# Hybrid RWKV-7 / short-convolution / expert block on one core: the w_o product in three f32r passes over blocks split as they arrive, and expert rows fetched two rounds ahead

## The reference, cut to what matters

```python
# 1024 tokens + 16 meta tokens = 1040 rows, D_MODEL 1024, 32 experts, top 4
x_n = _rmsnorm(h, ln1_g)
proj = x_n @ w_in
y_a = _rwkv7_branch(...)          # recurrence over 8 heads of 64
y_b = _short_conv_branch(...)
merged = sigmoid(gate_a) * y_a + sigmoid(gate_b) * y_b
h = h + merged @ w_o              # (1040, 1024) @ (1024, 1024)
xf = _rmsnorm(h, ln2_g)
logits = xf @ w_router + b_router
top_v, top_i = lax.top_k(logits, 4)
gates = softmax(top_v)
# per block of 128 rows that chose expert e:
gt = minimum(xb @ w_e_gate[e] + b_e_gate[e], 7)
up = clip(xb @ w_e_up[e] + b_e_up[e], -7, 7)
act = (up + 1) * (gt * sigmoid(1.702 * gt))
y = (act @ w_e_down[e] + b_e_down[e]) * wts
h = h + sum of the four y of each token
out = _rmsnorm(h, lnf_g)[16:]
```

## Time and profile before

| | us |
|---|---|
| median of 3 runs | 3091.75 (3083.33 to 3095.08) |
| the profiled execution | 3067.25 |
| its span in the profile | 3065.6 |
| PE busy | 2798.6 (91%) |
| DVE busy | 1789.7 (58%) |
| ACT busy | 1361.6 (44%) |
| POOL busy | 514.2 (17%) |

### The profile page before, as it was taken

How to read it: one execution, slowest core, us unless ns; L and a number is a source line. 1 busy time by engine, 2 the same in 40 slices (tenths; PEclk the granted TensorE clock), 3 DMA queues, 4 the chain that set the end, 5 groups by cost and what they waited for, 6 DMA issues and landing times.

```text
span 3065.6 us, 55893 instructions
## 1 busy us (share of the span) xinstructions
PE 2798.6 (91%) x21371; PEld 2340.7 (76%) x21371; DVE 1789.7 (58%) x1990; ACT 1361.6 (44%) x1501; POOL 514.2 (17%) x511
## 2 busy tenths in 40 slices
PE   7999999999998999796899999999899999999993
PEld 6797878878898999443688878888777777777772
DVE  3456546464422121143576776767788888888885
ACT  2423232232211111032565666665666666666664
POOL 1010101010000000123132323232222212222220
PEclk9999999999999999897899999999999999999996
DMA  3000000000012110522677868777988888988887
GB/s 105 21 2 15 8 8 15 2 22 1 28 41 56 41 41 21 156 67 70 230 280 257 282 248 283 257 281 264 352 324 323 323 327 330 353 331 329 327 331 245
DMA packets 143212, 536.25 MB, mean 175 GB/s; under 512 B 17633, under 2 KB 71239, under 8 KB 90125
## 3 DMA queue, kind: packets, MB, share of 16 engines
q1 hardware_dynamic: 122925, 492.74, 43.4%
q0 software_dynamic: 20192, 42.08, 5.6%
HBM read 500.35 MB, written 34.42 MB: 174 GB/s over the span
## 4 chain that ended last, share of the span: by engine, by line
PE 71%; DMA 14%; issue 7%; DVE 3%; POOL 2%; ACT 2%; POOLq 1%; SPq 0%; ACTq 0%; DVEq 0%
PE bank L839 30%; PE bank L1958 8%; PE bank L1959 7%; PE bank L1960 7%; DMA x_rows<-hn_d,next_t 6%; DMA next_t<-slot_d 5%; PE bank L1967 5%; PE bank L1871 4%; PE bank L1936 2%; PE bank L835 2%; POOL mid_t L1496 2%; PE bank L915 2%; DMA wo_t<-in_w_o 1%; PE bank L1946 1%; PE bank L2028 1%
## 5 line engine op out<-in xcount | busy, mean ns | idle before, releaser
L1789 DVE TENSOR_TENSOR w_lo<-raw_first,w_hi 128x2048 fp32r<-128x2048 f32 x275 | 618.3, 2283 | 73.7 <-ACT w_hi L1584 73.6
L1584 ACT ACTIVATE w_hi<-raw_first 128x2048 fp32r<-128x2048 f32 x276 | 529.5, 1919 | 228.1 <-DMA raw_first<-in_w_e_up 63.4
L1958 PE MATMUL bank<-w_hi,x_hi 128*128 128x512 f32 x1088 | 434.0, 399 | 2.4 <-ACT yo_rows L1632 2.4
L1959 PE MATMUL bank<-w_lo,x_hi 128*128 128x512 f32 x1088 | 425.1, 391 | 0.0
L1960 PE MATMUL bank<-w_hi,x_lo 128*128 128x512 f32 x1088 | 424.8, 390 | 0.0
L1789 DVE TENSOR_TENSOR w_lo<-raw_rest,w_hi 128x2048 fp32r<-128x2048 f32 x136 | 307.8, 2282 | 0.2
L1584 ACT ACTIVATE w_hi<-raw_rest 128x2048 fp32r<-128x2048 f32 x136 | 260.8, 1917 | 100.8 <-PE bank L1994 43.4
L839 PE MATMUL bank<-xm_hi,ring_hi 128*128 128x260 f32 x896 | 261.9, 292 | 16.2 <-DVE dz L791 8.2
L839 PE MATMUL bank<-xm_lo,ring_hi 128*128 128x260 f32 x896 | 255.0, 285 | 0.0
L839 PE MATMUL bank<-xm_hi,ring_lo 128*128 128x260 f32 x896 | 255.0, 285 | 0.0
L1958 PEld LDWEIGHTS bank<-w_hi,x_hi 128*128 128x128 f32 x1088 | 204.8, 188 | 51.2 <-issue 10.4
(11 more groups left out here) (364 smaller groups left out, 4706.3 us busy)
## 6 DMA issues: line engine op xcount, KB each, us to landing
raw_first<-in_w_e_up SPq DMA_DIRECT2D x138, 1024.0 KB, 5.9
raw_first<-in_w_e_gate SPq DMA_DIRECT2D x70, 1024.0 KB, 6.4
raw_rest<-in_w_e_gate SPq DMA_DIRECT2D x70, 1024.0 KB, 5.6
raw_first<-in_w_e_down SPq DMA_DIRECT2D x68, 1024.0 KB, 6.3
raw_rest<-in_w_e_down SPq DMA_DIRECT2D x68, 1024.0 KB, 8.7
ring<-in_w_in SPq DMA_DIRECT2D x40, 512.0 KB, 3.9
hn_d<-hn SPq DMA_DIRECT2D x10, 416.0 KB
h_d<-h_all SPq DMA_DIRECT2D x10, 416.0 KB
```

Source lines behind the costliest of these rows:

```text
L1584: nc.scalar.activation(w_hi[:, j % NRING, :, :], raw_piece(j), ACT.Copy).then_inc(hi_done, 1)
L1789: nc.vector.tensor_tensor(w_lo[:, j % NRING, :, :], raw_piece(j), w_hi[:, j % NRING, :, :].bitcast(f32), ALU.subtract).then_inc(lo_done, 1)
L1958: nc.tensor.matmul(ps[:, :], hi, w_hi[:, slot, k, :], start=start and k == 0, stop=False)
L1959: nc.tensor.matmul(ps[:, :], hi, w_lo[:, slot, k, :], start=False, stop=False)
```

## The change

- w_o: `mT` and w_o are both split in a high and a low f32r part, and `project_out` does three products for each of the eight channel blocks. w_o is split block by block (q = 0 to 15, a block is 128 channels by 512 columns); the first six blocks are loaded before the end of the gates into room that is free then, the other ten after it in two transfers ahead of `h_all`. ACT does the high parts (`split_wo_hi`, `split_m_hi`), DVE the low ones; those of tiles 2 to 9 of `mT` are done two tiles ahead, within the loop over tiles.
- The bias rows are laid out over 96 partitions (1024 elements each) in place of 32 (3072), and go out in six transfers in place of two.
- The padding (`make_pads`) is moved from the start of the w_o stage into the first `gather`, between the issue of the slot reads and the wait for them.
- `gather(1)` is done ahead of the loop, and in round r POOL does `gather(r + 2)`, behind the copy to `slot_t` and ahead of `get_biases(r + 1)` and the scatter. It waits for `xT_ps` of round r + 1.

```diff
+    WO_EARLY = 6
+    m_hi = wo("m_hi", [128, 2, KT, TP], f32r)
+    m_lo = wo("m_lo", [128, 2, KT, TP], f32r)
...
+        sp.dma_start(wo_early, w_o[:, 0:WO_EARLY, 0:512]).then_inc(wo_in[0], 16)
         sp.wait_ge(gate_mul, 3 * KT * NCH + 6)
-        sp.dma_start(wo_t[:, :, 0:512], w_o[:, :, 0:512]).then_inc(wo_in[0], 16)
+        sp.dma_start(wo_late[:, 0:KT - WO_EARLY, :], w_o[:, WO_EARLY:KT, 0:512]).then_inc(wo_in[1], 16)
+        sp.dma_start(wo_late[:, KT - WO_EARLY:, :], w_o[:, :, 512:1024]).then_inc(wo_in[2], 16)
         for t in range(NT):
-            if t == 2:
-                sp.dma_start(wo_t[:, :, 512:1024], w_o[:, :, 512:1024]).then_inc(wo_in[1], 16)
...
-        nc.gpsimd.memset(xo_rows, 0.0).then_inc(pads_done, 1)
-        nc.gpsimd.memset(bias_t.bitcast(f32), 0.0).then_inc(pads_done, 1)
...
         def gather(r, wide):
...
+            if isinstance(r, int) and r == 0:
+                make_pads()
             pool.wait_ge(idx_in[0], r * 16 + 16)
...
         gather(0, True)
         get_biases(0)
+        pool.wait_ge(rows_in[0], 16)
+        pool.wait_ge(rows_in[1], 16)
+        nc.gpsimd.tensor_copy(mid_t, next_t).then_inc(mid_kept, 1)
+        nc.gpsimd.tensor_copy(mid_ov, next_ov).then_inc(mid_kept, 1)
+        pool.wait_ge(mid_kept, 2)
+        pool.wait_ge(xT_ps[3], 1)
+        gather(1, True)
         pool.wait_ge(h_out, 16 * NT)
         for first, last, wide in ((0, n_wide, True), (n_wide, rounds, False)):
             with pool.Fori(first, last) as r:
-
-                pool.wait_ge(rows_in[0], r * 16 + 16)
...
-                pool.wait_ge(xT_ps[3 if wide else 1], r + 1)
-                gather(r + 1, wide)
...
+                pool.wait_ge(rows_in[0], r * 16 + 32)
...
+                pool.wait_ge(xT_ps[3 if wide else 1], r + 2)
+                gather(r + 2, wide)
...
+        act.wait_ge(gate_mul, 3 * KT * 4 + 6)
+        split_m_hi(0)
+        for q in range(KT):
+            split_wo_hi(q)
+        split_m_hi(1)
+        for q in range(KT, 2 * KT):
+            split_wo_hi(q)
...
             for k in range(KT):
-                ins = nc.tensor.matmul(bank[2 * (t % 2) + n][0:TP, :], mT[:, k, TP * t:TP * (t + 1)],
-                                       wo_t[:, k, 512 * n:512 * (n + 1)], start=k == 0, stop=k == KT - 1)
+                if t == 0:
+                    pe.wait_ge(wo_m_lo_done, WO_SPLITS['w', KT * n + k])
+                nc.tensor.matmul(ps, m_hi[:, t % 2, k, :], wo_hi[:, n, k, :], start=k == 0, stop=False)
+                nc.tensor.matmul(ps, m_hi[:, t % 2, k, :], wo_lo(KT * n + k), start=False, stop=False)
+                ins = nc.tensor.matmul(ps, m_lo[:, t % 2, k, :], wo_hi[:, n, k, :], start=False, stop=k == KT - 1)
```

## The result

The changed kernel takes 3007.63 us (median of 4 runs, 3003.55 to 3011.05), the kernel before 3087.54 (4 runs beside it on the same chip, 3081.65 to 3095.08). The ratio is 0.9739, with a 95% interval of 0.9711 to 0.9767: 80 us less, where 21 less was forecast. The two profiled executions lie closer together, 3067.25 and 3007.41, spans 3065.6 and 3005.8: 60 us.

A forecast was written before the change was run, and what follows sets the result against it. PE was taken as the bound in wide rounds, narrow rounds and w_o, stopping once a narrow round for x_rows. The terms -34 - 87 + 100 = -21 us on a median of 3091.75 gave 3071 us, range 2990 to 3140.

The forecast's parts named there:

- Narrow rounds, 87 forecast: Rows two rounds ahead remove the stall; less 0.3 us for biases and 0.6 for DMA, 4.1 us saved in 21 rounds.
- The stall: Narrow rounds: PE stops 3.34 us before x_part for x_rows, then loses 1.7 to low clock; 5.0 us a round.
- Wide rounds, 100 forecast: Biases read behind gather(r + 2) make PE stop 6.0 us, plus 1.7 of low clock; 7.7 us lost in 13 rounds.
- POOL's chain: Wide rounds, behind part f = 3: 1.5 us load, G 7.5, 1.5 expert load, 5.7 landing; 16.2 against 10.2 available.
- G: Time in POOL's wide-round chain for slot reads and both gathers: taken as 7.5 us, 6.0 at the least, 11.6 longest.
- rival 2: Wide rounds: next to no bias stop, small transfers land at once, rounds stay at 52 us; 2971 us, chance 0.07.
- Rival 1: Wide rounds: short bias stop of 3.2 us, G 6.0, costing 42 to 64 us; 3013 to 3035 us, chance 0.15.
- Rival 3: Wide rounds: POOL's chain with G 11.6 and landing 5.8, stop of 10.2 us, 171 lost; 3142 us, chance 0.16.
- Rival 4: Narrow rounds gain only 2 us, held at 39 by DMA or biases; 42 saved, 3116 us, chance 0.12.
- w_o, 34 forecast: w_o stage: tile 0's transposes 11 us earlier, then 17 halves saving 1.43 each, 24 us; 34 saved (28 to 40).
- its first low part at 1256.6: w_o start: half 1 waits for the second late transfer, there at about 1255.5; PE stops another 4 us.
- is covered by the next half of 5.4 and the logits, with over a us to spare: w_o tiles: the norm, some 5 us behind a tile's last product, stays hidden despite 0.9 us more DVE and ACT work.

The follow-up runs named there:

- the second pair of profiles: The kernel before and the changed kernel, both run again unaltered with profiles on the experiments' chips: 3066.69 us and 3017.8 us.
- the extra products: Changed kernel plus 18 f32r products that nothing reads, on PE in wide rounds before the wait for bias_t: 3003.03 us, ratio 0.9795.
- the w_o part alone: Kernel before plus the w_o work, bias layout and moved padding, with POOL's loop left one round ahead: 3044.14 us, ratio 0.9912.

## Why the prediction was right, and where its terms were off

The three mechanisms were there, each with its sign and at its place; the sizes were off, and most of each error has a name. Forecast was -34 - 87 + 100 = -21; on the chips of the experiments the whole is -50, in the first two profiles -60. So the way and the wide range of 2990 to 3140 came true, the size did not: 3007.63 lies below the 3035 to 3105 that the forecast itself was given. Two of the three errors point the same way, 26 us more from the narrow rounds and 18 less lost in the wide ones, and w_o, 9 short, took back a part of them.

**Narrow rounds, 87 forecast, 113 measured** (5.38 x 21; from the first product of round 13 on the two profiles differ by 112.6). The stall went with its full 5.0 us. I took off 0.3 for the biases and 0.6 for DMA at its limit; neither came. The DMA share is 1.00 and PE still runs every one of 600 us. The biases are issued some 7.1 us behind the slot read (2273.35 and 2266.26), while the sum for them had 7.8 + 1.0 + 1.5 = 10.3: the gather follows the slot read after 5.9 us instead of 7.8, and the load of the expert's number hardly shows. Why the slot read lands sooner isn't shown. The rest is the period itself. I took the one of the earlier trace rows, 40.95, and the mean over 20 rounds is 41.29.

**Wide rounds, 100 forecast, 81.5 measured** (83.0 in the second pair of profiles; 6.7 and 6.9 us a round). POOL's chain was 1.5 + 7.5 + 1.5 + 5.7 = 16.2. In the round shown it is 1.4 to the slot read's issue, 6.5 from there to the issue of the biases (1552.05 and 1558.53), which holds the load of the expert's number too, and 7.4 for the landing: 15.3, and a stop of 4.94. So G and the load, taken as 7.5 + 1.5 = 9.0, were the terms too large by 2.5: G was at its lower bound of 6.0, and the load lies mostly beside the gather's issue. The landing was 1.7 longer than the 5.7 I took and 1.3 longer than the longest of the earlier trace rows. The thirteenth read, for round 13, is needed in a narrow round and made PE wait only 1.3 us, so there were 12 stops to charge and not 13; their mean is (57.8 - 1.3) / 12 = 4.7 us. The clock cost what I took, 1.7: the extra products gave back 1.6 of it. Stop and clock together are 6.3 of the 6.7 us a round; the other 0.4 I can't place to one wait.

The Trainium skill (DMA: Bandwidth & Descriptors, Anatomy of one DMA), by which the biases would land in 2.06 us, is not what is mostly seen: they took 7.4 in the chain above, and rival 2 fell with it. One read, in round 11, did land after 2.31 us, near it, with no weights under way (last section). PE waited all the same, 7.3 us, since there the slot reads had taken the time. Rival 1 had the right G and too short a landing, 4.4. Rival 3's long gather came in that one round, 11.1 us from the slot read's issue to that of the biases; elsewhere it was 6.4 to 8.4. Rival 4 fell with the 5.4 us a round.

**w_o, 34 forecast, 24.8 measured** from the gates' end to the first product of the experts (22.6 in the second pair; 24.8 in time for the w_o part alone). The first product was expected 2.7 us behind the gates' end, and came so. Four things were short.
- The step "its first low part at 1256.6" was meant for gates ending at 1241.2, so 15.4 behind them. It came 17.1 behind (1254.41 against 1237.3), and half 0 was through 10.8 behind where I had 11.1: a stop of 6.35 us for 4. The transposes of tile 0 came 30.1 behind the gates' end for 28.3, 1.8 late.
- A half takes 24 x 0.230 = 5.5 rather than 5.44: 1 to 2 us in twenty halves.
- The norm "is covered by the next half of 5.4 and the logits, with over a us to spare" was the step that failed. I looked at ACT and DVE's load and not at their order. split_m_lo of t + 2 is ahead of choose of t - 1 on DVE, and PE's rank_tile waits for that choice: 0.91 us a tile from the fourth on. Of the 10.1 us in 6 waits shown above one is 5.6, at the last tile, where the kernel before has it too; the other five are 4.5 us, which is what the kernel with the step moved gets back.
- From the fourth tile on a tile is 0.23 us longer than the first ones even where PE waits for nothing (13.80 and 13.57), 1.4 us in six tiles. The cause isn't shown.

make_pads cost about 0.9 us, as taken (7.3 from the first slot read to its gather, 6.4 before).

**What stays open.** The kernel before took 3087.54 on the first chip and 3066.69 to 3069 on the others, while the changed kernel took 3007.63 there and 3017.8 here: one is 20 us longer, the other 10 shorter. The only trace from the first chip's kernel before is of an execution of 3067.25, that is one like those of the other chips, so what the runs near 3088 spent more isn't seen. Of the 10 us that the changed kernel was shorter, its two profiles (3005.8 and 3016.0) show 6.4 before the gates' end and 3.3 in the wide rounds, none in the narrow ones. 30 of the 80 us stand on such differences and not on the change. A forecast could not have had them, and the 50 of the other chips is the figure that the stages explain: the two profiles from chip 14 have -22.6 for w_o and the routing, +83.0 for the wide rounds and -110.0 from round 13 to the end, together -49.6, beside gates that end 5.1 us later in one of them.

## What to carry to other kernels

Requests that are moved on an engine's queue carry everything behind them along: ask what the next small, urgent read behind each is, and let the urgent one go first (here 74 us of 3018). Prefetch distance is a choice for each kind of round; where PE waits for no rows, an earlier request gains nothing and can meet other transfers. When new work is hidden by its amount, look at where in the order of that engine it is put, and who waits for the instruction behind it.

## What the runs showed of the hardware

- The 16 DMA engines at a share of 1.00 (381 GB/s over 600 us) held up nothing: PE was busy for 600.00 us of it. A share near one was not a limit with these buffers.
- A stop of some 5 us costs PE 1.6 us more in clock, and 4.24 us of products that nobody reads, put into it, keep the clock at 1.00 and gain 1.6 a round, though DMA still ends the wait.
- The f32r products of w_o were 0.230 us apart, as those of the rounds were within 0.003. With 104 rows in place of 128 a product is no shorter. The Trainium skill (TensorE: Matmul & The Clock Gate, Part 1) gives 0.216 for 512 columns; here each product has a new weight load beside it.
- One small read of biases lands 7.4 us after its issue where it stands behind the gather (chain above), and in 3.5 to 6.0 us in the wide rounds of the kernel that issues it first. In the round shown the SP queue had issued two pieces of weights of 1 MB each 1.9 us ahead of it:

```profile
1556.65 0.99 SPq L1392 DMA_DIRECT2D raw_rest<-in_w_e_gate  x2
```

Round 11 of the same execution has the same gathers in front of the read, the last one 1.2 us ahead, but the two pieces had been issued 10.4 us ahead, beside the slot reads. There the slot read took the time and the biases landed at once (start us, us, what, in the chain that ended last):

```profile
2081.97 6.84 DMA next_ov<-slot_d
...
2090.84 2.31 DMA bias_t<-bias_d
```

The second execution of the changed kernel, whose trace has the landings, says the same. In ten of its wide rounds 1 to 12 the biases land 0.2 to 0.4 us behind the second of the two pieces, 6.2 to 7.5 us after their issue; in round 7, with the pieces issued 5.7 and 5.0 us ahead, they take 4.2, and in round 11, where the pieces had landed before the read was issued, 2.3. So it is the weights under way that make a small read late, and not the gathers in front of it. No run moves the weights by themselves.
